# A hybrid attention, mLSTM and expert layer on one core: weights requested one stage later, the first tokens picked in bfloat16, and the last biases as stacked parts

## The reference

```python
px = split_cols(hx @ w_in, IN_SPLITS)      # one projection; 256 of its columns are the mLSTM queries "mq"
...
logits = (t @ router_w + router_b)         # 32 experts
top_logit, top_idx = lax.top_k(logits, 4)
gates = jax.nn.softmax(top_logit, axis=-1)
...
gu = xb @ w_gu[e] + b_gu[e]                # in blocks of the tokens of one expert
y = (glu * sigmoid(1.702 * glu) * (lin + 1)) @ w_down[e] + b_down[e]
x = x + g2 * sum_k gates[:, k] * y[expert k]
return rms_norm(x, final_norm_g)
```

## Time and profile before

| | us |
|---|---|
| median of 3 runs (2495.61 to 2496.01) | 2495.81 |
| the profiled execution | 2511.39 |
| its span | 2509.4 |
| TensorE busy | 2409.5 |
| VectorE busy | 1586.3 |
| ScalarE busy | 1087.2 |
| GpSimd busy | 520.7 |

### The profile page before, as it was taken

One profiled execution on the slowest core, in us unless ns is written; L12 is line 12 of the kernel. 1 busy time (PEld: TensorE's weight loads), 2 busy tenths in 40 slices (PEclk: granted clock), 3 DMA queues, 4 the chain that ended last, 5 costly groups with the idle time before them and its releaser, 6 DMA issues.

```text
span 2509.4 us, 34958 instructions
## 1 busy us (share of the span) xinstructions
PE 2409.5 (96%) x12254; PEld 1678.5 (67%) x12254; DVE 1586.3 (63%) x1914; ACT 1087.2 (43%) x1398; POOL 520.7 (21%) x493
## 2 busy tenths in 40 slices
PE   5999988999998879999999999999999999999998
PEld 3987764555557756676675778777767767767784
DVE  3332766676756767786786876555644644559994
ACT  3332334545453235564564564332422422437772
POOL 0000041656575021121111111110010110121111
PEclk8999999999998969999999999999999999999996
DMA  8450031000013467897987987888987987979993
GB/s 292 152 195 2 27 96 71 8 4 7 1 53 122 139 227 239 307 321 242 314 302 249 327 284 265 307 303 327 371 294 255 357 275 256 363 266 386 381 342 136
DMA packets 241045, 556.17 MB, mean 222 GB/s; under 512 B 27713, under 2 KB 32226, under 8 KB 239842
## 3 DMA queue, kind: packets, MB, share of 16 engines
q1 hardware_dynamic: 225296, 508.44, 56.4%
q0 software_dynamic: 12832, 46.27, 7.0%
q10 hardware_dynamic: 2834, 0.36, 0.1%
HBM read 519.66 MB, written 35.36 MB: 221 GB/s over the span
## 4 chain that ended last, share of the span: by engine, by line
PE 58%; DMA 1%; DVE 1%; issue 1%; ACT 1%; POOL 0%; DVEq 0%; ACTq 0%; POOLq 0%
PE PS L2284 29%; PE PS L2298 14%; PE PS L2279 6%; PE PS L2293 3%; DMA acc_dram<-y,idxs 1%; PE PS L2244 1%; PE PS L2255 1%; PE PS L2269 1%; PE PS L2374 1%; ACT wh L2426 1%; DVE wl L2533 0%; PE PS L2382 0%; PE PS L2385 0%; PE PS L2265 0%; DVE hid L2551 0%
## 5 line engine op out<-in xcount | busy, mean ns | idle before, releaser
L2533 DVE TENSOR_TENSOR wl<-w,wh 128x2048 fp32r<-128x2048 f32 x312 | 713.4, 2289 | 237.9 <-ACT wh L2426 236.9
L2426 ACT ACTIVATE wh<-w 128x2048 fp32r<-128x2048 f32 x312 | 597.8, 1916 | 404.8 <-PE PS L2284 298.6
L2284 PE MATMUL PS<-wh,xTh 128*128 128x512 f32 x1088 | 352.5, 405 | 0.0
L2284 PE MATMUL PS<-wl,xTh 128*128 128x512 f32 x1088 | 336.1, 390 | 0.0
L2284 PE MATMUL PS<-wh,xTl 128*128 128x512 f32 x1088 | 335.6, 390 | 0.0
L2179 POOL COPY idxg<-tokens 128x1 int32 (+1 forms) x47 | 29.4, 645 | 1053.7 <-PE PS L2244 980.4
L2284 PEld LDWEIGHTS PS<-wh,xTh 128*128 128x128 f32 x1088 | 200.8, 189 | 63.0 <-issue 21.1
L2284 PEld LDWEIGHTS PS<-wl,xTh 128*128 128x128 f32 x1088 | 204.5, 188 | 43.8
L2284 PEld LDWEIGHTS PS<-wh,xTl 128*128 128x128 f32 x1088 | 204.5, 188 | 43.3
L2279 PE MATMUL PS<-w,xTr 128*64 128x512 f32 (+1 forms) x1088 | 181.0, 519 | 0.0
L2298 PE MATMUL PS<-wh,hTh 128*128 128x512 f32 x544 | 178.3, 409 | 1.5 <-DVE hTl L2526 1.5
(11 more groups left out here) (438 smaller groups left out, 3552.9 us busy)
## 6 DMA issues: line engine op xcount, KB each, us to landing
w<-in_w_gu_dram SPq DMA_DIRECT2D x544, 512.0 KB, 11.4
w<-in_w_down_dram SPq DMA_DIRECT2D x136, 1024.0 KB, 12.4
later_wmod<-in_w_mod_dram SPq DMA_DIRECT2D x8, 2048.0 KB, 8.1
wmod<-in_w_mod_dram SPq DMA_DIRECT2D x8, 1024.0 KB, 14.3
x<-in_x_dram SPq DMA_DIRECT2D x8, 512.0 KB, 8.0
rowm<-rowm_dram SPq DMA_DIRECT2D x16, 256.0 KB, 3.3
w_out<-in_w_out_dram SPq DMA_DIRECT2D x1, 4096.0 KB, 12.7
ox<-in_x_dram SPq DMA_DIRECT2D x8, 512.0 KB, 4.1
```

Of the source, the lines that this page charges most:

```text
L2284: mm = pe.matmul(PS[:, b[g], :], x[part.n][:, k, :], ws[s][:, kk, g, :], start=False, stop=end and x is xTl)
L2426: act.activation(wh[c % SLOTS][:, :], w[c][:, :], ACT.Copy).then_inc(s_hi, 1)
L2533: dve.tensor_tensor(wl[c % SLOTS][:, :], w[c][:, :], wh[c % SLOTS][:, :].bitcast(F32), ALU.subtract).then_inc(s_lo, 1)
```

## The change

It has three parts.

1. The request for `w_mq` moves from the end of SyncE's list in modulation to the head of its list in projection.
2. In the route stage TensorE transposes the gates first and picks the first tokens after it. The selectors for the first tokens are bfloat16, in a place of their own; each token number is split into a lane (below 128) and a multiple of 128, both exact in bfloat16, so that there are 32 products of one column in place of 16 float32 ones. GpSimd makes `first_of` and two halves of `first_no`, three small operations for one.
3. For the final biases, `b_down` and the transposed gates are each fetched three times, into partitions 0 to 31, 32 to 63 and 64 to 95. GpSimd scales all 96 bias rows by g2. ScalarE rounds both to fp32r, behind its last weight chunk of the last visit, and VectorE replaces the middle 32 bias rows and the last 32 gate rows by what the rounding left over. One fp32r product over 96 partitions then gives high x high, high x low and low x high at once, in place of a float32 product over 32.

```diff
-                sp.dma_start(m.wMQ[:, :, :], w_all[:, :, C_MQ:C_MQ + 256]).then_inc(m.s_wA[KD + 1], 16)
...
+                w_all = a["w_in"].rearrange("l (k p) n -> p (l k) n", p=P)
+                sp.dma_start(m.wMQ[:, :, :], w_all[:, :, C_MQ:C_MQ + 256]).then_inc(m.s_wA[KD + 1], 16)
...
+        first_sel = m.at("first_sel", [P, 2, TX, P], BF16, end + 8 * TX * P)
-        first_sel = rowsel[:, 0:2 * TX, :].rearrange("p (c t) n -> p c t n", c=2)
+        first_sq = rowsel[:, 0:2 * TX, :].rearrange("p (c t) n -> p c t n", c=2)
...
-                pool.tensor_tensor(first_no[:, :], mask[:, :, 0], tok1, ALU.mult).then_inc(s_fn, 1)
+                pool.tensor_tensor(first_of[:, :], tok1, tok1[:, 0:1].to_broadcast([P, TX]), ALU.subtract).then_inc(s_fn, 1)
+                pool.tensor_tensor(first_no[:, :, 0], mask[:, :, 0], lane.to_broadcast([P, TX]), ALU.mult).then_inc(s_fn, 1)
+                pool.wait_ge(s_fn, 1)
+                pool.tensor_tensor(first_no[:, :, 1], mask[:, :, 0], first_of[:, :], ALU.mult).then_inc(s_fn, 1)
...
-                        ins = act.activation(first_sel[:, c, t, :], iota, ACT.Square, scale=-1.0, bias=first_at[:, c, t:t + 1])
+                        ins = act.activation(first_sq[:, c, t, :], iota, ACT.Square, scale=-1.0, bias=first_at[:, c, t:t + 1])
...
-                    act.activation(first_sel[:, c, :, :], first_sel[:, c, :, :], ACT.Relu, scale=-1.0, bias=ones[:, 0:1]).then_inc(s_fs, 1)
+                    act.activation(first_sel[:, c, :, :], first_sq[:, c, :, :], ACT.Relu, scale=-1.0, bias=ones[:, 0:1]).then_inc(s_fs, 1)
...
-                pe.wait_ge(s_fn, 1)
-                pe.wait_ge(s_fs, 2)
-                for c in range(2):
-                    for t in range(TX):
-                        mm = pe.matmul(PS[:, 3, 64 + c:65 + c], first_sel[:, c, t, :], first_no[:, t:t + 1], start=(t == 0), stop=(t == TX - 1))
-                mm.then_inc(s_fp, 1)
                 pe.wait_ge(s_gm, 1)
                 for t in range(TX):
                     mm = pe.matmul(PS[m.E, 4 + t // 4, (t % 4) * P:(t % 4 + 1) * P], m.gmat[:, t, :], m.ident[:, :], start=True, stop=True)
                 mm.then_inc(s_gt, 1)
+                pe.wait_ge(s_fn, 3)
+                pe.wait_ge(s_fs, 2)
+                for c in range(2):
+                    for t in range(TX):
+                        for i in range(2):
+                            mm = pe.matmul(PS[:, 3, 64 + c:65 + c], first_sel[:, c, t, :], first_no[:, t, i:i + 1], start=(t == 0 and i == 0), stop=(t == TX - 1 and i == 1))
+                mm.then_inc(s_fp, 1)
...
-                dve.tensor_scalar(first_tok[:, :], PS[:, 3, 64:66], -1.0, 0.0, ALU.add, ALU.max).then_inc(s_ft, 1)
+                dve.tensor_scalar(first_tok[:, :], PS[:, 3, 64:66], 0.0, None, ALU.max).then_inc(s_ft, 1)
...
-        bdn = m.at("bdn", [P, D], F32, W0 + 4 * 8192 + 4096)
+        braw, graw = m.at("bdn_raw", [96, D], F32, HIDDEN_AT + 4096), m.at("gT_raw", [96, TX, P], F32, HIDDEN_AT + 12288)
+        bparts, gparts = m.at("bdn_parts", [96, D], F32R, x_at + 4096), m.at("gT_parts", [96, TX, P], F32R, x_at + 12288)
...
+        s_gd, s_bk, s_gk = sem("gate_rows_in"), sem("down_bias_parts"), sem("gate_parts")
...
-                sp.dma_start(bdn[E, :], a["b_down"].rearrange("l e n -> (l e) n")).then_inc(s_bd, 16)
+                for r in range(0, 96, NE):
+                    sp.dma_start(braw[r:r + NE, :], a["b_down"].rearrange("l e n -> (l e) n")).then_inc(s_bd, 16)
+                for r in range(0, 96, NE):
+                    sp.dma_start(graw[r:r + NE, :, :], gT[E, :, :]).then_inc(s_gd, 16)
...
+                pool.wait_ge(s_bd, 48)
+                pool.wait_ge(s_gb, 16)
+                pool.tensor_tensor(braw[:, :], braw[:, :], g2bc[0:96, :], ALU.mult).then_inc(s_bg, 1)
...
-                        pe.matmul(PS[:, s + g, :], gT[E, t, :], bdn[E, 512 * g:512 * g + 512], start=True, stop=False)
+                        pe.matmul(PS[:, s + g, :], gparts[:, t, :], bparts[:, 512 * g:512 * g + 512], start=True, stop=False)
...
-                pe.wait_ge(s_bg, 1)
+                pe.wait_ge(s_bk, 2)
+                pe.wait_ge(s_gk, 2)
...
-                def visit(v, parts, before, following, banks, next_split):
+                def bias_parts():
...
+                    act.wait_ge(s_bg, 1)
+                    act.activation(bparts[:, :], braw[:, :], ACT.Copy).then_inc(s_bk, 1)
+                    act.wait_ge(s_gd, 48)
+                    act.activation(gparts[:, :, :], graw[:, :, :], ACT.Copy).then_inc(s_gk, 1)
...
+                def visit(v, parts, before, following, banks, next_split, last=False):
...
+                    if last:
+                        bias_parts()
...
-                visit(n1 + NV, SPILL, 2 * n1 + 6 * NPAIR, None, None, False)
+                visit(n1 + NV, SPILL, 2 * n1 + 6 * NPAIR, None, None, False, last=True)
...
-                dve.wait_ge(s_bd, 16)
-                dve.tensor_tensor(bdn[E, :], bdn[E, :], g2bc[E, :], ALU.mult).then_inc(s_bg, 1)
+                dve.wait_ge(s_bk, 1)
+                dve.tensor_tensor(bparts[NE:2 * NE, :], braw[NE:2 * NE, :], bparts[NE:2 * NE, :].bitcast(F32), ALU.subtract).then_inc(s_bk, 1)
+                dve.wait_ge(s_gk, 1)
+                dve.tensor_tensor(gparts[2 * NE:, :, :], graw[2 * NE:, :, :], gparts[2 * NE:, :, :].bitcast(F32), ALU.subtract).then_inc(s_gk, 1)
...
```

More of the change, by code:

```diff
@@ L1827, in phase_route @@
             ("codei", [P, TK], I32), ("coli", [P, TK], I32), ("lanei", [P, TK], I32),
-            ("colf", [P, TK], F32), ("lanef", [P, TK], F32),
+            ("colf", [P, TK], F32), ("lanef", [P, TK], F32)])
+        first_sel = m.at("first_sel", [P, 2, TX, P], BF16, end + 8 * TX * P)
+        more, end = m.run(end, [
             ("rowsel", [P, TK, P], F32), ("colsel", [P, TK, NBLK], F32), ("pairs", [P, TK, 2, NBLK], F32),
@@ L1834, in phase_route @@
             ("capcol", [P, 2, NE], F32), ("jump", [P, NE], F32),
-            ("first_at", [P, 2, TX], F32), ("first_no", [P, TX], F32), ("first_tok", [P, 2], I32)])
+            ("first_at", [P, 2, TX], F32), ("first_of", [P, TX], F32), ("first_no", [P, TX, 2], BF16), ("first_tok", [P, 2], I32)])
         (ones, upper, gt, gsum, ohc, resets, gpair, rank, tot, over, nb, b1, b0, code, codei, coli, lanei,
          colf, lanef, rowsel, colsel, pairs, b1d, b1c, cmp_t, nbi, ohg, blk, tokf, empty, zeros, key, above, place,
-         plan, expm, expr, visitm, capcol, jump, first_at, first_no, first_tok) = items
-        first_sel = rowsel[:, 0:2 * TX, :].rearrange("p (c t) n -> p c t n", c=2)
+         plan, expm, expr, visitm, capcol, jump, first_at, first_of, first_no, first_tok) = items + more
+        first_sq = rowsel[:, 0:2 * TX, :].rearrange("p (c t) n -> p c t n", c=2)
         assert end <= 193440
```

## The result

| us | before | after |
|---|---|---|
| timed beside each other, 6 runs each: median | 2495.91 (2493.72 to 2500.02) | 2487.31 (2485.33 to 2492.64) |
| profiled execution | 2511.39 | 2492.42 |
| span | 2509.4 | 2490.3 |

The ratio is 0.9961 [0.9944, 0.9979], so -8.6 us where -22.3 was forecast. The two profiled executions lie 19.0 apart. The clue is in that pair of numbers: the profiled execution of before lay 15.6 above its median, that of after only 5.1. For the profiled execution the forecast was 2489.1, and 2492.42 was measured; it is the step from there to the median that went wrong.

A forecast was written before the change was run, and what follows sets the result against it. TensorE, busy 96% of the span, was taken as the bound. Start -2.4, route -1.1 and final stage -18.8 made -22.3 us: 2489.1 profiled, 2473.5 median with the 15.6 difference carried over; range 2467.5 to 2481.5.

The forecast's parts named there:

- the term of -18.9: Final stage: six tile periods each shortened by 3.14 us, from TensorE's 5.71 to six products taking 2.57.
- The start, -2.4: Border of modulation and projection: without w_mq's request the next stage starts at 32.2; ends 0 and -2.4 us.
- The route, -1.1 (ends -2.9 and +2.1): Route stage: last first-token result at 900.9 instead of 902.03 us, from earlier transposes and 32 bfloat16 products.
- the product of one column: Route stage: each of 32 products costs its bfloat16 weight load, taken as 0.117 us, 3.7 us in all.
- The slip of 1.0 on VectorE: Route stage: `plan` waits behind GpSimd's added operations, moving VectorE's arrival at the first-token wait from 899.13 to 900.1 us.
- The first add, -2.8: Final stage: single-pass bias products end before `yl`, so the first `add` comes at 2461.0 instead of 2463.81 us.
- The period, 5.71 to 2.72, -18.0 with the +0.9: Final stage: period per tile 2.72 us, ends 2.57 and 3.5; the +0.9 allows for GpSimd steps unable to run beside `scale`.
- From the last `add` to the end nothing changes: Tail of the final stage: stays 9.6 us after the last `add`, which was at 2499.77.
- the lag of two tiles: Final stage: slack said to absorb GpSimd's five small operations per tile, keeping the period near 2.57 rather than 3.5 us.
- GpSimd's scaling, +2.0: Last visit: scaling 96 x 1024 takes 2.4 us and delays VectorE's second `wl`; ends 0 and +2.4 us.
- (a): Rival, final stage: GpSimd and VectorE together bound it at 3.5 us per tile, +4.7, so 2478.2; chance 0.18.
- (d): Rival, first visits: TensorE's clock stays at 0.50 after the route; 60 us of it gives 2503.5, slower; chance 0.03.

The follow-up runs named there:

- part 2: Kernel before with only the route's bfloat16 selectors and gate transposes in front: 2492.94 us, ratio 1.0003 [0.9981, 1.0025]; clock stayed up in its profile.
- part 3: Kernel before with only the stacked biases and the rest of the final-bias change, nothing of start or route: 2493.81 us against 2496.42, ratio 0.9987.
- the three sets: Twelve follow-up kernels, four per set, each set on one chip beside 35 runs of the kernel before; no single time.
- part 1: Kernel before with only w_mq's request moved from modulation to projection: 2492.95 us, ratio 0.9993 [0.9968, 1.0018].
- parts 1 and 2: Kernel before with the moved request and the route change, final stage as before: 2495.40 us, ratio 0.9994 [0.9972, 1.0016].
- the second comparison: Changed kernel once more, no edit, twelve runs beside the kernel before: 2491.17 us against 2498.91, ratio 0.9960 [0.9942, 0.9977].

## Why the prediction was wrong

The step that failed is the step from the profiled execution to the median, and with it the term of -18.9. I read a period of 5.71 us and a clock of 0.50, worked out what it would become, and carried the difference of 15.6 over to the median unchanged. The 15.6 us were the very thing that the change removes, and the median of before never had them. Six periods of 5.71 instead of 3.03 are 16.1 us; with the first tile and the tail, the profiles of before and of part 2 differ by 18.6 between `y` and the last scaling. Against the profiled execution the sum held (-22.3 forecast, -19.0 measured), though its terms did not all; against the median part 3 was worth next to nothing (-2.6 timed, alone). Over the three sets 20 of 154 runs with the final stage of before (the kernel before itself, part 2, part 1, parts 1 and 2) have a mean granted clock of 0.974 or less and mostly lie some 12 to 20 us above their medians; of the 60 runs with the stacked biases none does, nor of the 12 without bias products.

Point by point:

- **The start, -2.4**: right at the border (projection begins at 34.54 to 34.94 in seven profiles without part 1, at 32.16 to 33.11 in seven with it), and the medians of where the route begins are 885.1 and 881.5. Single profiles scatter by 2 to 3 us there (883.67 to 885.64, 881.08 to 884.31). In the profile of after no engine waits for a weight to land in projection.
- **The route, -1.1 (ends -2.9 and +2.1)**: it is -3.3, because `first_tok` no longer waits for TensorE at all. From VectorE's first operation of the stage to ScalarE's first `wh` of the experts it takes 38.6 us in the profile of before (37.7 in two of the others without part 2) and 35.3 in the median of the seven with part 2. The mis-sized term is the product of one column: I took 0.117, the longest record of a bfloat16 load, and they start 0.03 apart (0.95 us for 32). A record's length isn't the distance to the next, and the earlier trace rows had it: float32 records of 0.333 that start 0.218 apart. The slip of 1.0 on VectorE didn't come either: `gpair` started 0.3 later in the stage instead of 0.6, `plan` shrank from 0.83 to 0.34, the 0.71 of `expm` beside `gmat` took its place, and VectorE was at `first_tok` 15.2 us into the stage instead of 15.3. The clock there was at 1.00, where before had 0.50 over its own products (895 to 902 us); how much of the short pitch that is, no run shows:

```profile
894.80:895.80 1.00, 1.00 (x33) 0.87 (x32) 0.97 (x2) 0.85 (x1) 0.00 (x0) 1.00 1.03 410
```

  The Trainium skill, "TensorE: Matmul & The Clock Gate", section "LDWEIGHTS", gives the columns over 1.2 in ns, so 107 ns for 128. The records come near (95 to 99 ns), the pitch of 0.03 us does not: such loads overlap here, and the estimate worked out from that figure would have been wrong by nearly the same factor as mine.
- **The first add, -2.8**: it stands at 2461.1 as forecast. But before's own 2463.81 belonged to the rare execution. From `y` to the first add it is 6.43 there, 4.69 with the clock up (part 2's profile) and 3.48 with the stacked biases: -1.2.
- **The period, 5.71 to 2.72, -18.0 with the +0.9**: it is 3.03 to 2.93, and as the first tiles and the tail count too, from first add to last scaling 24.32 became 24.82, a little longer. "From the last `add` to the end nothing changes" was wrong too: it is 12.0 for 9.6, since each of the last two scalings waits 1.65 for its root. The bound I named was right in kind (GpSimd's steps can't run beside a scaling with two SBUF inputs) and wrong in size: I let the lag of two tiles take it up. It can't, because `var` is the first link of the loop: it comes up just as the scaling starts (2465.43 and 2465.38), stands still, 1.29 in all, and Ln, Exp and four steps follow before the next scaling may start. Taking `var` out of that loop gave 2.47, which is VectorE's own work. The one number that I could have summed from the rows, 1.28 + 0.45 + 1.1, makes 2.8.
- **GpSimd's scaling, +2.0**: with the rest of the new work 2.1 in the profile of after, 0.6 in four others.
- **The rivals**: (a) named the right pair of engines; at 3.5 it overrated them. (d), the clock, looked at the wrong place: I said that in the final stage it was at the lower level already, and took one execution's level for the kernel's. In the first visits the clock did what it had done before, only earlier (at 1.00 from 926 to 960, where before has it from 931 on).

So part 3 in a run whose clock stays up is about -1.2 + 0.5 + 0.6 by the profiles, next to nothing (alone it timed -2.6, [0.9977, 0.9997]), and some -16 in the one in eight whose clock falls. Parts 1 and 2 make -2.4 and -3.3. The sum, -5.8, stands against -8.6, whose interval (-14 to -5.2) holds it, and, without the runs that have the step, -6.4 in the second comparison.

What stays open is a stretch of the experts. Four pairs of visits, between 1585 and 1842 us, took 254 to 263 us from profile to profile, while no other step from scatter to scatter differs by more than 0.5 us. The six profiles with parts 1 and 2 have 256.4 to 262.0 there (mean 259.4), the eight others 253.6 to 263.0 (mean 256.3). In one of these pairs in after, the scatters at 1666.35 and 1685.05 lie 3.1 us further apart than before. The trace shows late weights there. ScalarE waits 1.65, 2.96 and 1.72 us for three chunks of w_gu, where in before it waits 0, 0.33 and 3.85. The second of them, in after and in before:

```profile
1676.94 1.91 ACT L2443 ACTIVATE wh<-w 128x2048 fp32r<-128x2048 f32 x1 [2.96 <-DMA w<-in_w_gu_dram]
```

```profile
1677.70 1.92 ACT L2426 ACTIVATE wh<-w 128x2048 fp32r<-128x2048 f32 x1 [0.33 <-DMA w<-in_w_gu_dram]
```

TensorE is idle for 3.2 us around it (1666 to 1688), where before has 1.1 (1671 to 1690), and its clock drops to 0.50 for 3.4 us. All seven profiles with such a drop in this stretch took 257.2 us or more for it, the seven without one 256.4 or less; five of the six with parts 1 and 2 have one, two of the eight others. Whether the earlier start makes the chunks late, or that is chance, these runs don't settle; nothing was tried on it.

## What to carry to other kernels

When a profiled execution lies far from the median of the timed runs, find the difference in it before working anything out, and above all don't scale a saving by what that execution shows: a stage at PEclk 0.50 in one profile may be at 1.00 in most runs. A second profile of the same kernel may show the rare case again, as it did here; the timed runs, and the profile of another kernel with the same stage, told it. For each stage work out the time at either level of the clock, and what bounds it when TensorE no longer does: here one column of GpSimd work as the first link of a loop cost more than the products that were made faster. A small operation that depends on another engine's small operation is best given what it needs directly, as the logarithm was.

## What the runs showed of the hardware

- The granted clock can fall while TensorE is busy without a gap. During the first eight float32 products over 32 rows it went from 1.00 to 0.50 in three of the five profiles with the final stage of before, and once more in the kernel with 24 of them (15.41 us); over 128 rows of other data, with the same number of products in the same place (10.46 us), it stayed. Whether eight of them do it, and whether it comes back in 4 us or not before the end (period 3.03 or 5.71), differs from execution to execution.
- One-column products with 128 x 128 bfloat16 weights start 0.03 us apart at the level of 2.4 GHz, load included; their load records are 0.095 to 0.099 long.
- Where GpSimd and a VectorE operation with two SBUF inputs meet, one keeps the other waiting for its whole instruction, however small that one is: one column of `var` took 1.28 to 1.30 instead of 0.19, an operation over 128 x 8 took 1.09 instead of 0.2, and the scaling of 96 x 1024 took 2.40 or 4.05 to 4.37, with VectorE's `wl` pair at 6.82 or 4.57. Mostly it is the later one that waits, but not always by the records' starts: `rowsel` in the earlier trace rows starts 0.23 us ahead of the first of three `pairs` and ends 1.09 us behind the last. Beside `add`, which reads PSUM, GpSimd's steps keep their 0.19.
